# Two of three norms: rows scaled in SBUF and transposed, in place of products with a diagonal

## The reference

```
x += 1/2 * g1 * SwiGLU_1(modulate(rms_norm(x), sh1, sc1))
h  = modulate(rms_norm(x), sh2, sc2);  z = h @ w_in      (mLSTM and attention branches)
x += g2 * mix
x += 1/2 * g3 * SwiGLU_2(modulate(rms_norm(x), sh3, sc3))
rms_norm(x) = x * rsqrt(mean(x*x) + eps) * w;  modulate(h, shift, scale) = h * (1 + scale) + shift
```

## Time and profile before

| | |
|---|---|
| median of 3 runs | 2226.61 us (2225.94 to 2227.69) |
| profiled execution, its own time | 2227.96 us |
| its span in the profile | 2226.0 us |
| TensorE busy | 2196.0 us, 99% |
| VectorE, ScalarE, GpSimd busy | 1628.4, 937.6, 64.5 us |
| mean granted TensorE clock | 0.998 |

### The profile page before, as it was taken

How to read it: one execution, slowest core, us unless ns; L and a number is a source line. 1 busy time by engine, 2 the same in 40 slices (tenths; PEclk the granted TensorE clock), 3 DMA queues, 4 the chain that set the end, 5 groups by cost and what they waited for, 6 DMA issues and landing times.

```text
span 2226.0 us, 28370 instructions
## 1 busy us (share of the span) xinstructions
PE 2196.0 (99%) x10466; PEld 1755.8 (79%) x10466; DVE 1628.4 (73%) x1881; ACT 937.6 (42%) x1098; POOL 64.5 (3%) x55
## 2 busy tenths in 40 slices
PE   6999999999999999999999999999999999999999
PEld 3567777777777778888888888888888888888887
DVE  3446888888888889756867888985567676776856
ACT  3343333333333336455544344454444444344443
POOL 0001000000000000000600000100000000000000
PEclk9999999999999999999999999999999999999999
DMA  9998898888888876654536776846665757557563
GB/s 362 371 368 302 286 316 302 280 282 299 315 281 290 283 255 219 220 173 158 195 106 235 259 256 234 276 162 207 226 237 190 264 188 264 188 191 261 188 228 131
DMA packets 273332, 548.13 MB, mean 246 GB/s; under 512 B 9014, under 2 KB 9418, under 8 KB 273008
## 3 DMA queue, kind: packets, MB, share of 16 engines
q1 hardware_dynamic: 212676, 423.69, 55.9%
q10 hardware_dynamic: 57484, 113.47, 14.2%
q0 software_dynamic: 3104, 10.05, 1.5%
HBM read 543.71 MB, written 3.46 MB: 246 GB/s over the span
## 4 chain that ended last, share of the span: by engine, by line
PE 94%; DVE 3%; DMA 1%; issue 1%; ACT 1%; SPq 0%; DVEq 0%; ACTq 0%
PE ps L701 29%; PE ps L703 29%; PE ps L702 29%; PE ps L638 1%; PE ps L623 1%; DMA ada_w_sb<-in_ada_w 1%; PE ps L778 1%; DVE w_lo L1801 1%; PE ps L688 0%; DVE acc L2015 0%; PE ps L1103 0%; PE ps L1171 0%; PE ps L1179 0%; DVE xm L1921 0%; ACT w_hi L1350 0%
## 5 line engine op out<-in xcount | busy, mean ns | idle before, releaser
L1350 ACT CAST w_hi<-raw_w 128x1024 fp32r<-128x1024 f32 x728 | 766.2, 1054 | 1158.3 <-PE ps L703 1116.6
L1801 DVE TENSOR_TENSOR w_lo<-raw_w,w_hi 128x1024 fp32r<-128x1024 f32 x728 | 897.1, 1236 | 409.2 <-ACT w_hi L1350 405.9
L701 PE MATMUL ps<-w_hi,xT_hi 128*128 128x512 f32 x2080 | 822.2, 395 | 5.8 <-DVE xT_lo L1889 4.5
L703 PE MATMUL ps<-w_hi,xT_lo 128*128 128x512 f32 x2080 | 811.3, 390 | 0.0
L702 PE MATMUL ps<-w_lo,xT_hi 128*128 128x512 f32 x2080 | 810.8, 390 | 0.0
L701 PEld LDWEIGHTS ps<-w_hi,xT_hi 128*128 128x128 f32 x2080 | 391.1, 188 | 111.3 <-issue 25.3
L703 PEld LDWEIGHTS ps<-w_hi,xT_lo 128*128 128x128 f32 x2080 | 391.0, 188 | 83.3
L702 PEld LDWEIGHTS ps<-w_lo,xT_hi 128*128 128x128 f32 x2080 | 391.3, 188 | 78.7
L1861 DVE SCALAR_TENSOR_TENSOR vec_acc<-ada_w_sb,ctile,vec_acc 128x512 f32<-128x512 f32 x420 | 299.2, 746 | 0.0
L701 PE MATMUL ps<-w_hi,hT_hi 128*128 128x512 f32 x704 | 276.4, 393 | 0.0
L703 PE MATMUL ps<-w_hi,hT_lo 128*128 128x512 f32 x704 | 274.2, 390 | 0.0
(11 more groups left out here) (279 smaller groups left out, 1044.4 us busy)
## 6 DMA issues: line engine op xcount, KB each, us to landing
raw_w<-in_ffn_wi SPq DMA_DIRECT2D x176, 1024.0 KB, 5.1
ada_w_sb<-in_ada_w ACTq DMA_DIRECT2D x96, 1024.0 KB, 8.3
raw_w<-in_ffn_wo SPq DMA_DIRECT2D x88, 1024.0 KB, 5.3
raw_w<-in_w_in SPq DMA_DIRECT2D x68, 1024.0 KB, 5.3
ada_w_sb<-in_ada_w SPq DMA_DIRECT2D x30, 1024.0 KB, 13.1
raw_w<-in_w_out SPq DMA_DIRECT2D x16, 1024.0 KB, 5.3
ada_m<-in_ada_w ACTq DMA_DIRECT2D x12, 1024.0 KB, 5.4
raw_w<-in_w_proj_m SPq DMA_DIRECT2D x8, 1024.0 KB, 5.2
```

Source lines behind the costliest of these rows:

```text
L701: pe.matmul(out, a_hi, w_hi[:, slot, kk, :], start=(first and kk == 0), stop=False)
L703: mm = pe.matmul(out, a_lo, w_hi[:, slot, kk, :], start=False, stop=(last and kk == 1))
L1350: act.copy(w_hi[:, us % SPL, :, :], raw_w[:, slot, 2 * half:2 * half + 2, :]).then_inc(hi_ready, 1)
L1801: dve.tensor_tensor(w_lo[:, us % SPL, :, :], raw_w[:, slot, 2 * half:2 * half + 2, :], w_hi[:, us % SPL, :, :].bitcast(F32), ALU.subtract) ...
```

## The change

For the second and third norm the diagonal is gone. VectorE multiplies columns 0 to 1023 of a group's rows of `x` by the inverse root, in two instructions of 512 columns, and ScalarE columns 1024 to 2047 in one Copy with the same column as scale. Both write to `acc`, which is free then. TensorE transposes the blocks of `acc` with its transpose mode. Its steps 0, 2 and 4 of a group wait for the three pieces. Since `acc` is used, GpSimd clears it for the second FFN only after the last transpose of the third norm, behind its `gate_load(1)`. The first norm keeps the diagonal (its semaphore has a new name).

```
# GpSimd
             pool.wait_ge(mix_ready, NCH)
-            pool.memset(acc[:], 0.0).then_inc(acc_done, 1)
             pool.wait_ge(units_done, U_OUT)
             pool.wait_ge(gate_stored, 32)
             gate_load(1)
+            pool.wait_ge(norm_ps, norm_done(2, LAT, 7))
+            pool.memset(acc[:], 0.0).then_inc(acc_done, 1)
             pool.wait_ge(gate_rows_ready, FCH)
# TensorE, norm(s)
-                    pe.wait_ge(diag_ready, 2 * s + g + 1)
                     for j in range(8):
+                        if j in (0, 2):
+                            pe.wait_ge(xn_dve, 4 + 2 * part(s, g) + j // 2 + 1)
+                        if j == 4:
+                            pe.wait_ge(xn_act, 4 + part(s, g) + 1)
...
-                            mm = pe.matmul(ps[:, j, b * TOK + g * P:b * TOK + (g + 1) * P],
-                                           x[:, g, k * P:(k + 1) * P], diag[:, g, :], start=True, stop=True)
+                            mm = pe.transpose(ps[:, j, b * TOK + g * P:b * TOK + (g + 1) * P], acc[:, g, k * P:(k + 1) * P], ident)
# ScalarE
+            def scaled(s, g):
+                act.wait_ge(rscale_ready, 2 * s + g + 1)
+                act.activation(acc[:, g, 2 * CH:], x[:, g, 2 * CH:], ACT.Copy, scale=small[:, 14 + g:15 + g]).then_inc(xn_act, 1)
...
                 sumsq(s, 3, LAT)
                 root(s, LAT)
                 modulate(3, CTX)
+                scaled(s, LAT)
                 modulate(5, CTX)
...
                     root(1, CTX)
+                    scaled(1, CTX)
                     split(U_IN + 1, 0)
...
             root(2, CTX)
+            scaled(2, CTX)
             for n in range(AHEAD):
                 split(U_F2 + n, 0)
# VectorE
+            def scaled(s, g):
+
+                dve.wait_ge(root_ready, 2 * s + g + 1)
+                dve.reciprocal(small[:, 14 + g:15 + g], small[:, 12 + g:13 + g]).then_inc(rscale_ready, 1)
+                dve.wait_ge(rscale_ready, 2 * s + g + 1)
+                for n in range(2):
+                    c = slice(n * CH, (n + 1) * CH)
+                    dve.tensor_scalar(acc[:, g, c], x[:, g, c], small[:, 14 + g:15 + g], None, ALU.mult).then_inc(xn_dve, 1)
...
-                diagonal(s, LAT)
+                scaled(s, LAT)
...
-                        diagonal(1, CTX)
+                        scaled(1, CTX)
...
-            diagonal(2, CTX)
+            scaled(2, CTX)
             split(U_F2, 0)
```

More of the change, by code:

```diff
@@ L302, in build @@
         ada_sel_done, ada_cols_done = sem("ada_sel_done"), sem("ada_cols_done")
-        sumsq_ready, var_ready, root_ready, diag_ready = sem("sumsq_ready"), sem("var_ready"), sem("root_ready"), sem("diag_ready")
+        sumsq_ready, var_ready, root_ready, rscale_ready = sem("sumsq_ready"), sem("var_ready"), sem("root_ready"), sem("rscale_ready")
         gT_ps, gT_ready, ada_blk_ready, ada_T_done = sem("gT_ps"), sem("gT_ready"), sem("ada_blk_ready"), sem("ada_T_done")
@@ L350, in build, with part @@
         state_stored, kv_stored, sink_arg = sem("state_stored"), sem("kv_stored"), sem("sink_arg")
+        def part(s, g):
+            return 2 * (s - 1) + g
         def norm_done(s, g, j):
@@ L676, in norm @@
                             k = 2 * j + b
-                            mm = pe.matmul(ps[:, j, b * TOK + g * P:b * TOK + (g + 1) * P],
-                                           x[:, g, k * P:(k + 1) * P], diag[:, g, :], start=True, stop=True)
+                            mm = pe.transpose(ps[:, j, b * TOK + g * P:b * TOK + (g + 1) * P], acc[:, g, k * P:(k + 1) * P], ident)
                         mm.then_inc(norm_ps, 1)
             def norm0(banks):
-                pe.wait_ge(diag_ready, 2)
+                pe.wait_ge(rscale_ready, 2)
                 for j in banks:
@@ L1879, in diagonal @@
                 chain(dve.reciprocal(small[:, 14 + g:15 + g], small[:, 12 + g:13 + g]))
-                dve.tensor_scalar(diag[:, g, :], ident, small[:, 14 + g:15 + g], None, ALU.mult).then_inc(diag_ready, 1)
+                dve.tensor_scalar(diag[:, g, :], ident, small[:, 14 + g:15 + g], None, ALU.mult).then_inc(rscale_ready, 1)
+            def scaled(s, g):
[5 more added lines that the diff above has]
+                    dve.tensor_scalar(acc[:, g, c], x[:, g, c], small[:, 14 + g:15 + g], None, ALU.mult).then_inc(xn_dve, 1)
             def xn_copy(n):
```

## The result

The changed kernel takes 2231.70 us in the median of 20 executions (2229.09 to 2235.23), the kernel before 2226.15 (2224.63 to 2227.69): ratio 1.0025, 95% interval 1.0019 to 1.0031, slower by 5.5 us. The forecast was 2234.3. Its profiled execution took 2232.78 with a span of 2230.8 and a mean granted clock of 0.995, where before had 0.998. Two later executions of the kernel before, of 2753 and 4485 us, were disturbed and are left out.

What follows compares the result with a forecast made beforehand. At the norms VectorE's queue, not TensorE's products, was taken to bound the kernel. 2226.6 + 2.4 (queues) + 5.3 (two clock falls) = 2234.3 us, slower by 0.35%, chance 0.55; range 2228.0 to 2237.0.

Steps and rivals of the forecast that it cites:

- The queues: Second and third norm: longer VectorE and ScalarE work delays the first product by 1.05 and 1.33 us, +2.4 in sum.
- VectorE's pair: Two 128x512 multiplications by a column per group: 0.80 us, net +0.59 after removing the diagonal.
- the wait for `y_read`: Third norm: TensorE waits for it in front of block 3, which costs it nothing yet.
- TensorE's own work: Per norm, transposes replacing products with the diagonal cut TensorE's work from 7.6 to about 3.8 us.
- on the path that is worth nothing: Both norms: TensorE's saved 3.8 us only becomes idle time while VectorE and ScalarE set when `xT_hi` and `xT_lo` come.
- Moved: GpSimd's clearing of `acc` (3.52 us) goes from 1393.82 to about 1491 and costs nothing itself; `gate_load(1)` comes 3.5 us earlier.
- The clock: Both norms: TensorE's clock falls to 0.50 after 8.9 us without products, 2.65 us a fall, +5.3 us in all.
- that case: If much of the low clock falls into the wait and not on products, a fall costs less, down to 1.3 us.
- The rival with one fall: The clock falls at one norm only: 2226.6 + 2.4 + 2.7 = 2231.7 us; chance 0.07.
- the forecast's own range: Whole kernel: 2231.5 to 2237.0 us around the forecast 2234.3.
- The reason: Clock at both norms: transposes don't count as work as products do, and half of the 8.9 us stretch is idle.
- The pause ahead of the first product: Second norm: TensorE pauses 1.6 us after the latents' sixteen transposes, which are spread to 867.7.

Runs made afterwards that it cites:

- half by half: Kernel before with only the context's rows scaled and transposed, 2227.33 us, ratio 1.0006; with only the latents' rows so, 2227.30 us, ratio 1.0008.
- The transposes by themselves: Kernel before, diagonal still made and waited for, but TensorE transposes the unscaled rows in transpose mode: 2226.31 us, ratio 1.0001.
- the two fillings: Changed kernel with useless products in TensorE's pauses at both norms, 2228.75 us, ratio 1.0011; only ahead of the latents' transposes, 2228.28 us, ratio 1.0008.
- half the products under both queues: One product per step, not two: in the kernel before, 2226.53 us, ratio 1.0002; in the changed kernel, with identity products replacing transposes, 2230.25 us, ratio 1.0022.

## Why the prediction came out as it did

**The queues: right.** Forecast +1.05 and +1.33, measured +0.98 and +1.26, and half by half 1.0 and 1.2 for context and latents. VectorE's pair took 0.80 as forecast, the Copy 1.04 to 1.06 for 1.05, and at the cast (865.59, without a wait) ScalarE was the last. The Copy loaded no table. Two slips don't bear on the sum: 867.95 for 866.88 is +1.07 and not +1.05, and the wait for `y_read`, put at nothing, is 0.96 us of TensorE's time at the third norm, though off the path.

**TensorE's own work: right in size, not quite right in worth.** 32 records a norm, one every 0.115, and no gain in this kernel. But "on the path that is worth nothing" overlooked ScalarE's wait for step 1. The transposes by themselves bring the first product forward by 0.51 and 0.18 us; the Copy ahead of that step takes it back.

**Moved: right.** The clearing cost nothing.

**Between the norms: not forecast.** The prediction stopped at each norm's first product. The 0.9 us that are lost 236 us behind the second one, at the attention's keys, stand in no term of it.

**The clock: it fell, but for half of the reason given, and the term was too large.** The fall came, to the level forecast, in the first trace at both norms. The forecast had 2 x 2.65 = 5.3 us; by the times it is 5.5 - 2.24 - 0.9 = 2.4, less than half. Two numbers in it were off. A fall cost 1.77 and 2.16 in the first trace and 1.81 in the second (4.66 behind its third norm less 2.85 behind its second), since it begins in the pause and a part of it is over before products come; I had named that case and put it aside. And it doesn't come twice at full length in each execution: 10 of 30 have the mean clock of the trace with two falls, 3 that of the kernel before. The rival with one fall (2231.7 us) has the median to the digit, but partly by luck: it adds 2.4 and 2.7 to 2226.6, and measured are 2.24, 0.9 and 2.4 on 2226.15. That the median lies within the forecast's own range, at its lower edge of 2231.5, is luck in the same way: without the 0.9 it would be 2230.8.

The reason had two parts. That transposes don't hold the clock, so that 8.9 us without a product lower it, was wrong: 7.8 us without one held in 11 of 11 executions, and products failed with nearly the same pauses. That half of the stretch is idle was right: the two fillings, and half the products under both queues, show that the pauses decide. The pause ahead of the first product, forecast at 1.6, is 1.37 where the clock holds.

By mean clock the sums close too. Queues and the third loss make 3.1, and the executions at 0.998 lie 2.9 above before; with the 3.9 of two falls in the first trace it is 7.1, and those at 0.995 lie 7.0 above.

**What stays open.** Which property of the pauses counts isn't settled: the longest of them doesn't tell, and with the same 2.28 us pause the clock fell at the second norm in one trace and not in the other. Whether transposes bring a low clock back up wasn't run. The cause of the later load is open, and the third loss is read from one trace of each kernel (two of the changed one). Nor was it tried to scale the rows on an engine that is free.

## What to carry to other kernels

An engine whose work is halved gains nothing where it wasn't awaited, and TensorE can pay for the idle time with its clock at the next dense stretch: pauses of at most 2.3 us, in stretches that were thin around them, cost up to 2.2 us a norm here. Before work is moved from TensorE to VectorE and ScalarE, look which of the three is last at the handover, and add up what is queued behind the new instructions there. Where the time of a kernel spreads more than that of its neighbour, set each execution's time beside its granted clock. And lay the two traces beside each other past the edited places: here 0.9 us were lost 236 us behind one.

## What was unexpected of the hardware

Transposes held TensorE at 2.4 GHz for 7.8 us without a product (11 executions). Products making up the same occupation didn't, once the pauses among them were longer (2.19 us at the second norm, 1.43 at the third; 0.995 to 0.998 in 11 executions). The same program, with the same waits to 0.01 us up to the point where the clock falls, shows two falls in one execution and one in the other. VectorE's subtraction of 128x1024, 1.23 us elsewhere, took 3.09 with 2.01 us of a GpSimd multiplication beside it; GpSimd's clearing of 128x4096 beside another subtraction cost nothing.
